# ScalarE's copies of the inverse's diagonal blocks, written ahead of the next chunk's high split

## What is computed

```python
kb = k * beta[..., None]
a_mat = jnp.where(strict, jnp.einsum('bhnid,bhnjd->bhnij', kb, k) * decay, 0.0)
t_mat = lax.linalg.triangular_solve(a_mat + eye, eye, left_side=True, lower=True)
u = t_mat @ (v * beta[..., None])
w = t_mat @ (kb * jnp.exp(gc)[..., None])
...
def chunk_step(S, xs):
    v_new = u_n - w_n @ S
    o_n = q_n @ S + intra_n @ v_new
    S = S * jnp.exp(gl_n)[..., None, None] + jnp.einsum('bhcd,bhce->bhde', k_n, v_new)
```

## Time and profile before

| | |
|---|---|
| median of 3 runs | 2887.15 us (2886.69 to 2887.62) |
| the profiled execution | 2887.95 us, its span 2886.1 us |
| busy, of the span | PE 99%, PE weight loads 96%, DVE 62%, ACT 49%, POOL 5% |
| DeltaNet stage | up to about 900 us, 16 turns of about 52 us |

### The profile page before, as it was taken

One profiled execution on the slowest core, in us unless ns is written; L12 is line 12 of the kernel. 1 busy time (PEld: TensorE's weight loads), 2 busy tenths in 40 slices (PEclk: granted clock), 3 DMA queues, 4 the chain that ended last, 5 costly groups with the idle time before them and its releaser, 6 DMA issues.

```text
span 2886.1 us, 68598 instructions
## 1 busy us (share of the span) xinstructions
PE 2845.7 (99%) x25415; PEld 2763.0 (96%) x25415; DVE 1777.9 (62%) x2837; ACT 1425.7 (49%) x2189; POOL 136.2 (5%) x268
## 2 busy tenths in 40 slices
PE   8999999999999999999999999999999999999999
PEld 7989899899888999999999999999999999999999
DVE  7778788787785455555555444587555555554444
ACT  6656566565664344444444433566444444444443
POOL 1111111111110000000000000000000000000000
PEclk9999999999999999999999999999999999999999
DMA  7666656656555555555555555744455555555554
GB/s 224 185 181 182 189 169 188 183 171 190 163 180 179 195 188 179 181 181 178 179 181 179 181 180 183 220 154 133 168 178 180 182 179 178 181 182 180 180 181 147
DMA packets 521089, 518.90 MB, mean 180 GB/s; under 512 B 32127, under 2 KB 444200, under 8 KB 520664
## 3 DMA queue, kind: packets, MB, share of 16 engines
q1 hardware_dynamic: 519150, 510.29, 56.5%
q0 software_dynamic: 1152, 5.58, 0.6%
q10 hardware_dynamic: 594, 0.25, 0.0%
HBM read 492.06 MB, written 32.82 MB: 182 GB/s over the span
## 4 chain that ended last, share of the span: by engine, by line
PE 67%; ACT 1%; DMA 0%; DVE 0%; issue 0%; SPq 0%; DVEq 0%; ACTq 0%; POOLq 0%
PE bank L505 11%; PE bank L510 11%; PE bank L506 11%; PE upper L505 11%; PE upper L510 10%; PE upper L506 10%; PE upper L1034 0%; DMA x_res<-x_spill 0%; PE upper L1059 0%; PE upper L1045 0%; DMA out_dram<-S 0%; PE upper L1096 0%; DVE s_dec L2432 0%; PE upper L1172 0%; PE upper L1035 0%
## 5 line engine op out<-in xcount | busy, mean ns | idle before, releaser
L484 DVE TENSOR_TENSOR w_lo<-w_raw,w_hi 128x1024 fp32r<-128x1024 f32 x858 | 1050.7, 1225 | 923.6 <-ACT w_hi L477 920.6
L477 ACT ACTIVATE w_hi<-w_raw 128x1024 fp32r<-128x1024 f32 x858 | 908.7, 1059 | 1230.9 <-PE bank L510 696.5
L505 PE MATMUL bank<-h_hi,w_hi 128*128 128x264 f32 x3168 | 829.3, 295 | 1.6 <-ACT w_hi L477 1.3
L506 PE MATMUL bank<-h_lo,w_hi 128*128 128x264 f32 x3168 | 794.2, 284 | 0.0
L505 PEld LDWEIGHTS bank<-h_hi,w_hi 128*128 128x128 f32 x3168 | 596.7, 188 | 25.1 <-issue 9.0
L506 PEld LDWEIGHTS bank<-h_lo,w_hi 128*128 128x128 f32 x3168 | 597.8, 189 | 0.9
L510 PE MATMUL bank<-h_hi,w_lo 128*128 128x264 f32 x3168 | 449.8, 284 | 0.0
L510 PEld LDWEIGHTS bank<-h_hi,w_lo 128*128 128x128 f32 x3168 | 412.6, 188 | 0.0
L505 PE MATMUL upper<-h_hi,w_hi 128*128 128x264 f32 x1456 | 361.7, 285 | 0.0
L506 PE MATMUL upper<-h_lo,w_hi 128*128 128x264 f32 x1456 | 361.4, 284 | 0.0
L505 PEld LDWEIGHTS upper<-h_hi,w_hi 128*128 128x128 f32 x1456 | 274.3, 188 | 0.0
(11 more groups left out here) (441 smaller groups left out, 3611.0 us busy)
## 6 DMA issues: line engine op xcount, KB each, us to landing
w_raw<-in_w_gate_up_dram SPq DMA_DIRECT2D x704, 256.0 KB, 2.9
w_raw<-in_w_in_a_dram SPq DMA_DIRECT2D x388, 256.0 KB, 3.2
w_raw<-in_w_down_dram SPq DMA_DIRECT2D x352, 256.0 KB, 2.9
w_raw<-in_w_out_a_dram SPq DMA_DIRECT2D x128, 256.0 KB, 3.2
s_dec<-in_state_delta_dram SPq DMA_DIRECT2D x32, 512.0 KB, 6.2
out_dram<-s_dec SPq DMA_DIRECT2D x32, 512.0 KB, 5.0
w_raw<-in_w_q_b_dram SPq DMA_DIRECT2D x64, 256.0 KB, 3.2
w_raw<-in_w_o_b_dram SPq DMA_DIRECT2D x64, 256.0 KB, 2.9
```

What stands on the lines that cost most here:

```text
L477: nc.scalar.activation(w_hi[:, s % SPL, :], w_raw[:, s, :], ACT.Copy).then_inc(hi_ready, 1)
L484: ops.tensor_tensor(w_lo[:, s % SPL, :], w_raw[:, s, :], w_hi[:, s % SPL, :].bitcast(F32), ALU.subtract).then_inc(lo_ready, 1)
L505: nc.tensor.matmul(bank[bk][:, 0:T], high(t), xh, start=first, stop=False)
L506: nc.tensor.matmul(bank[bk][:, 0:T], high(t), xl, start=False, stop=False)
```

## The change

ACT's two copies to the diagonal blocks belong to step 12, which stands behind the high split of chunk 7. They become step 11, which is the end of the round before, so they stand ahead of that split. Their wait (inv_pe 9) and the semaphore that they raise stay.

```diff
-                elif n == 12:
+                elif n == 11:
 
                     act.wait_ge(inv_pe, 12 * G + 9)
                     for b in range(2):
                         at = slice(HP * b, HP * (b + 1))
                         m = nc.scalar.activation(UF[at, :, at], Um[at, :, :], ACT.Copy)
                     m.then_inc(inv_act, 1)
```

## The result

| | before | changed |
|---|---|---|
| median | 2887.13 us (2886.69 to 2887.62, 4 runs) | 2870.64 us (2869.59 to 2871.47, 4 runs) |
| profiled execution, its span | 2886.1 us | 2869.7 us |

The ratio is 0.9941, with a 95% interval of 0.9928 to 0.9953: 16.5 us less, where 15.8 were forecast, and 2870.6 against 2871.3 us. In a later series, 5 runs of the changed kernel had a median of 2871.21 us beside 14 of the kernel before with 2887.32.

A forecast was written before the change was run, and what follows sets the result against it. PE was taken to bound the kernel, so only its pauses at line 2011 could yield time: 16 x 0.99 = 15.8 us off the median of 2887.15 gives 2871.3 us, with a range of 2868 to 2875.

The forecast's parts named there:

- The bound and the place: PE is busy 99% of the span; time can come only from its pauses, 15.5 us of them at line 2011.
- The releaser: At line 2011 the transpose of line 2376 (end 410.55) releases PE, not the profile's copy of line 1725 (410.56).
- The copies: ScalarE's copies of line 1721 run from 406.10 to 406.93, inside 3.09 us of idle time, with 0.88 us to spare.
- VectorE: Line 2373 needs only line 2001's matmuls and starts at 408.15; the transpose ends at 409.07 instead of 410.55.
- PE and the sum: Line 2011 starts at 409.67 without a pause, saving 0.99 us per group, 15.8 us over 16 groups.
- What is next late: Line 2379's copy comes 1.48 us earlier, at 410.64; PE's margin at line 2020 grows from 0.61 to 1.10 us.
- The slower rival: Chunk 7's split comes too late and PE pauses there: 2903 at 2 us past a margin of 4.1 us; chance 3%.

The follow-up runs named there:

- The half of the turns: Kernel before, with the two copies ahead of the split in every second turn of ACT's loop, 7 of 16 groups: 2880.16 us, ratio 0.9976.
- The delays: Changed kernel with 1, 2, 3 or 4 extra ACT copies of 128 x 1024 ahead of the two copies: 2871.1, 2877.5, 2898.7, 2938.1 us.
- N = 2: Changed kernel with two extra ACT copies of 128 x 1024 between the wait for line 1993 and the two copies: 2877.5 us.
- the square first: Kernel before, with ACT's square of line 1727 put ahead of the copy of line 1725: 2887.24 us, ratio 1.0000.
- N = 4: Changed kernel with four extra ACT copies of 128 x 1024 between the wait for line 1993 and the two copies: 2938.1 us.

## Why the prediction was right, point by point

**The bound and the place.** PE's pauses at line 2011 were the whole of it, and they went whole. The half of the turns showed that each is worth its own microsecond.

**The releaser.** The reading of the program against the profile's row held: the run with the delayed copy of line 1725 shows PE starting 0.67 us before it. Without that reading the forecast would have been the same number with a wrong reason.

**The copies.** Forecast: from 406.10 to 406.93, a wait for line 1993 of about 1.4 us, the split of chunk 7 unmoved with 0.88 us to spare. Measured, on the same clock: 406.11 to 406.95, 1.39 us, 407.81 and 0.85 us.

**VectorE.** Forecast: line 2373 at 408.15, the transpose's end at 409.07. Measured: 408.22 and 402.85 + 0.30 + 5.98 = 409.13. The signal from line 2001 took 0.14 us instead of 0.07; the margin of half a microsecond took it.

**PE and the sum.** Line 2011 was forecast at 409.67 and started at 403.69 + 5.98 = 409.67. The passage without a wait is 0.33 us, and so its row at line 1993 (0.34) was the right one to take for a 64x64 tile as well. The range was wider than it had to be on this account: the profile of before has 64x64 tiles in line 1918 too, whose weight loads start 0.33 us behind the last one of line 506, without a wait (the last two of these four lines, from the kernel before):

```profile
433.16 0.19 PEld L506 LDWEIGHTS bank<-h_lo,w_hi 128*128 128x128 f32 x1
433.50 0.74 PEld L2099 LDWEIGHTS upper<-norm_sq,masks 128*128 128x128 f32 x4 [0.15 <-issue]
...
445.25 0.19 PEld L506 LDWEIGHTS bank<-h_lo,w_hi 128*128 128x128 f32 x1
445.58 0.32 PEld L1918 LDWEIGHTS upper<-Pb,PbT 64*64 64x64 f32 x16
```

The idle 0.15 us ahead of line 2011 is still there (403.69 - 403.36 - 0.19 = 0.14), without any wait in the profile, so the 18.4 us of the weight-load row, the end of the range at 2868.7, was too much.

The Trainium skill (TensorEngine Tiling (Array Packing), Key Properties) says that a switch of tiling mode drains TensorE. The 0.14 us doesn't contradict it, but that the drain is its cause isn't shown. Line 2099 above has the same 0.15 us ahead of it, with 128x128 tiles on both sides, and the switches back to 128x128 behind lines 1993 and 2011 have only 0.04 and 0.07 us.

The gain up to the last line 2011 was 16.2 us, 16 x 1.01, against 16 x 0.99; the 0.3 us between that and the medians' 16.5 lie within the scatter of single runs (2869.59 to 2871.47).

**What is next late.** Forecast: line 2379's copy ends at 410.64, with 1.10 us of margin at line 2020. Measured: 404.73 + 5.98 = 410.71, and 405.72 - 404.73 = 0.99 us.

**The slower rival.** This is the one point that was thought out wrongly. I had put its margin at 4.1 us, up to the moment where PE wants the high half of chunk 7. The delays show the margin that counts to be that of the transpose. In the changed kernel the copies end at 400.97 us and may end 1.24 us later, 0.03 us ahead of line 2373's start at 402.24. From the transpose's release of PE at 403.15 + 0.11 = 403.26 to PE's own arrival at 403.69 there are 0.43 us more, which makes 1.67 us in all, the margin that the doses gave. One extra copy (1.06 us) cost nothing, two (2.15) cost 6.3 us, three made it slower than before. I had that chain in the sum, and left it out of the rival. And the price of a miss isn't only the pause: with pauses of 1.5 us and of 2.6 us the clock added to it.

## What to carry to other kernels

On an engine that runs its program in order, look for an instruction whose input is ready while the engine idles at the one ahead of it: here 0.8 us of copies stood behind a wait of 3.1 us, and exchanging the two cost nothing and gave 1 us in each of 16 turns. The margin of such a move is that of the shortest chain that hangs on the moved work, here 1.7 us over VectorE to TensorE, not that of the instruction it was moved past. When a wait's named releaser ends within hundredths of a microsecond of another engine's instruction, read in the program which semaphores it waits for.

## What the runs showed of the hardware that I had not expected

The clock reacts to short pauses in otherwise busy work, and the more often the longer they are. In the DeltaNet stage none of the 16 pauses of 0.4 us (N = 2) had a granted clock below 1.00 behind it, and none of the 57 of 1.0 us (16 each before, with the square first and with the delayed copy, 9 with half of the turns). Of 16 pauses of 1.5 us, 3 had about 3 us at the 1.2 GHz level behind them. Of 16 pauses of 2.6 us, 14 had one, three of them for about 7 us. For N = 4 that costs some 26 us on top of 41 us of pauses.

The pause needn't be a repeated one. Some 40 us behind the last turn's step 13 PE waits once for VectorE's low split (line 510), and the length of this wait differs between the profiled executions. In four of the twelve it was 0.88 to 1.99 us, and the clock stayed at 1.00 behind it. In eight it was 2.04 to 3.32 us, and in six of these about 3 us at the 1.2 GHz level followed. It is 2.41 us in the profile before and 2.15 in the one after, each with such a stretch; the 0.26 us between them are about what the gain grows by behind the last line 2011, from 16.2 to 16.4 us.

The Trainium skill (TensorE: Matmul & The Clock Gate, Part 1: The HAM clock gate) has the same two levels and gives idleness as the cause. The runs agree with both: the clock is at 0.50 in the stretches behind the pauses, and the counts above grow with the pause.
